# Hybrid decoder trunk: a pooled chunk moved two places, squares one chunk later, the convolution branch by column halves, attention outputs split straight from PSUM

## The chip, the cores and the metric

The kernel runs on one core of a Trainium2 chip. The metric is the time of one execution in microseconds (us), taken on the device; the figure for a kernel is the median of its runs. Beside the times there is one profiled execution, with a trace of every instruction.

## The reference

Two layers, each of a token mixer, a cross-attention into 256 memory tokens and a channel mixer (a dense SwiGLU in layer 0, a top-2-of-8 mixture of experts in layer 1); 256 tokens of width 1024, all float32. The change lies in the mixer and the attention:

```python
proj = xn @ w_in + b_in                       # conv a, b; pool; q, k, v, z; i, f; three gates
u = causal_depthwise_conv(c_a * sigmoid(c_b), conv_dw_w, conv_dw_b)      # 31 taps
y_a = silu(layer_norm(u, g, b)) @ w_conv_out
y_b = pool_mixer(p_u, pool_w, pool_scale) @ w_pool_out                   # 4 groups, each @ pool_w[g]
h = mlstm_chunkwise(q, k, v, ig, lf)                                     # 4 heads
h = h * rsqrt(mean(h * h) + EPS) * mlstm_norm_g                          # the second norm
y_c = (h * sigmoid(m_z)) @ w_mlstm_out
y = g[0] * y_a + g[1] * y_b + g[2] * y_c
x = x + y @ w_out
x = x + concat_heads(softmax(q @ k.T / 16) @ v) @ wo                     # cross-attention
```

## The kernel before

Everything is held transposed, with channels on the 128 partitions and the 256 tokens along the free dimension. Products keep float32 accuracy in three passes: each operand is split into a high part (rounded to the matmul's format) and a low part (what is left), and the helper `three` issues high by high, high by low and low by high.

The weights stream in chunks of 2048 columns per partition (1 MB). SyncE loads chunk c into `raw[c % 3]`; ScalarE copies it to `w_hi[c % 3]` (line 662, once TensorE has finished chunk c-3); VectorE subtracts to get `w_lo[c % 3]` (line 1017, the helper `lo`); TensorE multiplies it in 48 matmuls. The pooled chunk ("pw", four 128x128 blocks) has 512 columns and 12 matmuls.

The list `MIX` sets the order of the 63 chunks of a layer, the same on every engine. ScalarE and VectorE both run the loop "`split(c)`, then `post(c - 3)`", so the low part of chunk c stands in each queue ahead of all that follows from chunk c-3. The queues run strictly in order: a wait in a `post` holds up the splits behind it. The chunk numbers that matter (before): pu1 17, k3 18, z1 to z3 19 to 21, pw 22, gb0 to gb3 (gates) 23 to 26, wp0 and wp1 (pool output) 27 and 28, gc0 29, ga3 40, wc0 and wc1 (convolution output) 41 and 42, wo0 to wo3 43 to 46, xv3 58, xo0 59.

Beside the splits the queues carry:

- `conv31` on VectorE: the 31-tap convolution, doled out by the table `TAPS` over the chunks (line 1083, two instructions for each tap).
- `hidden(hd)` on VectorE, in the `post` two chunks after the scores of head hd (`SCORES` = 11, 15, 19, 23), scales the numerators into `q_t`; `hidden_squares(hd)` on ScalarE, in the same `post`, waits for it and squares `q_t` (line 733). In `post(26)` ScalarE takes the root of the sums (line 807) and VectorE normalises `q_t` (lines 1220 and 1222). `hidden_transpose` on TensorE (line 1617) comes after gc0.
- The pooled chunk: `pooling` in `post(17)` on VectorE; in `post(PW - 2)` ScalarE copies the pooled sums to `b_hi` (line 798) and VectorE makes `b_lo`, for which TensorE waits ahead of pw; in `post(PW)` VectorE scales the product (line 1210), ScalarE copies it (line 801), VectorE makes `b_lo`, and wp0 uses it.
- `merge` on VectorE: gate times branch. For wp it writes `xf` (line 1135) and frees the PSUM bank that gc0 takes. For wc it multiplies and adds (lines 1137 and 1138) once the whole chunk is done; ScalarE makes `a_hi` (line 749) and VectorE `a_lo` (`merged_lo`, signal `y_lo`). A wc chunk has four blocks of 128 rows of its input and fills two banks; wo0 reads `a_lo` in four steps of two blocks each and waits at each step for one `y_lo`.
- Attention: `x_output(hd)` on TensorE (line 1654) writes bank 7; it waits for the value chunk's copy `xv_done` (`x_value`, line 1147, which comes first in the `post`) and for `xo_done`, the copy of the previous head out of bank 7 (`x_out`, line 1162). ScalarE makes `a_hi` (line 769), VectorE `a_lo`. Heads 2 and 3 both come after xv3.

PSUM banks 0 to 3 go round by `bank_plan`; who takes a bank waits until it has been read.

Of the kernel before, what the change touches and what calls it, by code (L numbers as in the profile page):

```python
# [26 lines left out]
P = 128  # L27
T = 256
# [25 lines left out]
MIX += [("q", 2), ("z", 0), ("k", 2), ("pu", 0), ("q", 3), ("pu", 1), ("k", 3), ("z", 1), ("z", 2), ("z", 3), ("pw", 0)]  # L54
MIX += [("gb", i) for i in range(4)] + [("wp", i) for i in range(2)]
# [63 lines left out]
SCORES = (11, 15, 19, 23)  # L119
GATE_ROWS = AT["q", 0]  # L120
# [5 lines left out]
MEM_STEPS = (0, 1, 3)  # L126
CONSTS = 9
# [56 lines left out]
def trunk(nc, w, out):  # L184
    ctx = ExitStack()
    with ctx:
# [6 lines left out]
        def sig(name, mixer, ffn=0, before=0):  # L193
            return Signal(ctx, nc, name, mixer, ffn, before)
# [167 lines left out]
        ln_lo = sig("ln_lo", 1, before=1)  # L362
        y_done = sig("merged", 4)
# [16 lines left out]
        xo_done = sig("x_out_copied", HEADS)  # L380
# [273 lines left out]
        def _(act):  # L654
# [238 lines left out]
            def mixer(layer):  # L893
                if layer == 0:
                    first_norm()
                else:
                    for j in range(4):
                        act.wait_ge(h_ff.sem, h_ff.at(layer, j - 3))
                        square(layer, 0, j)
                    std(layer, 0)  # L900
# [16 lines left out]
                ahead(layer, SPL - 1)  # L917
# [94 lines left out]
        def _(dve):  # L1012
# [113 lines left out]
            def merge(layer, j, n, parts):  # L1126

                multiplied(layer, j)
                for i in range(parts):
                    dve.wait_ge(gate_done.sem, gate_done.at(layer, n + i + 1))  # L1130
                    s, q = 2 * ((n + i) % 4), (n + i) % 4
                    g, y = flat(gates[:, s:s + 2, :]), flat(xf[:, 2 * q:2 * q + 2, :])
                    last = y_done if n >= 8 else gate_used
                    if n < 4:
                        dve.tensor_tensor(y, g, bank(("chunk", j), i)[:, :], ALU.mult).then_inc(last.sem, 1)
                    else:
                        ch.link(dve.tensor_tensor(g, g, bank(("chunk", j), i)[:, :], ALU.mult))
                        dve.tensor_tensor(y, y, g, ALU.add).then_inc(last.sem, 1)
# [33 lines left out]
            def post(layer, j):  # L1172
# [45 lines left out]
                if j == SCORES[-1] + 3:  # L1218
# [100 lines left out]
            def mixer(layer):  # L1319
# [196 lines left out]
        def _(pe):  # L1516
# [141 lines left out]
            def chunk(layer, c):  # L1658
# [304 lines left out]
```

## Time and profile before

| | us |
|---|---|
| median of 3 runs (2160.7 to 2167.48) | 2162.11 |
| profiled execution, its time | 2162.14 |
| profiled execution, span of the core | 2160.3 |
| TensorE busy | 2059.6 |
| VectorE busy | 1637.2 |
| ScalarE busy | 1299.9 |

The span runs from the first to the last instruction in the trace, and the time of the same execution is 1.8 us longer. TensorE is busy in 95% of the span; its mean granted clock is 0.978 of full speed. The two mixers with their attention lie at 15 to 464 us and 664 to 1111 us.

### The profile page before, as it was taken

The numbers are of one execution on the slowest core, as the hardware profiler recorded it, in microseconds if no ns is written. First come the engines' busy times: TensorE is split into PE (matmuls) and PEld (weight loads), VectorE is DVE, ScalarE is ACT, GpSimd is POOL, SyncE is SP. The second block draws the span as 40 slices with busy tenths as digits, with TensorE's granted clock in tenths as the row PEclk, the third lists the DMA queues.
The fourth block names the chain that finished last, engine by engine and source line by source line (L and its number), as shares of the span: only waits on it lengthen the run. The fifth ranks groups of instructions, "written<-read, shape, count | busy, mean of one in ns | idle before, by whom it ended". The sixth has DMA issues, their size and how long they took to land.

```text
span 2160.3 us, 33554 instructions
## 1 busy us (share of the span) xinstructions
PE 2059.6 (95%) x12929; PEld 1871.5 (87%) x12929; DVE 1637.2 (76%) x1704; ACT 1299.9 (60%) x1133; POOL 13.2 (1%) x71
## 2 busy tenths in 40 slices
PE   8998999999998998989979999999999999999996
PEld 8988989889998988989878888888888888888885
DVE  6988656554446888656559888888988888898885
ACT  6664354343334664454337777777777777777774
POOL 0000000000000000000000000000000000000000
PEclk9998999999999999999989999999999999999998
DMA  8544445435554545445437999999999999999892
GB/s 248 176 124 161 132 155 176 151 117 181 190 176 145 167 124 161 135 152 175 139 136 285 385 325 376 330 366 353 354 373 331 376 332 367 343 366 373 328 377 91
DMA packets 309518, 526.76 MB, mean 244 GB/s; under 512 B 13566, under 2 KB 156582, under 8 KB 309414
## 3 DMA queue, kind: packets, MB, share of 16 engines
q1 hardware_dynamic: 309414, 525.29, 69.7%
q8 instruction: 75, 1.23, 0.2%
q14 instruction: 29, 0.24, 0.0%
HBM read 524.21 MB, written 1.05 MB: 243 GB/s over the span
## 4 chain that ended last, share of the span: by engine, by line
PE 80%; DVE 9%; issue 4%; ACT 4%; SPq 1%; PEldq 0%; DMA 0%; PEld 0%; DVEq 0%; ACTq 0%; POOL 0%
PE ps L1519 25%; PE ps L1521 24%; PE ps L1520 24%; DVE w_lo L1017 2%; DVE c L1083 2%; ACT w_hi L662 2%; PE ps L1839 1%; ACT w_hi L669 1%; PE ps L1913 1%; PE ps L1634 1%; DVE cacc L1067 1%; PE ps L1566 1%; PE ps L1654 1%; PE ps L1901 0%; PE ps L1902 0%
## 5 line engine op out<-in xcount | busy, mean ns | idle before, releaser
L1017 DVE TENSOR_TENSOR w_lo<-raw,w_hi 128x2048 fp32r<-128x2048 f32 x330 | 752.5, 2281 | 368.4 <-ACT w_hi L662 304.4
L1519 PE MATMUL ps<-w_hi,a_hi 128*128 128x512 f32 (+1 forms) x1472 | 566.1, 385 | 0.6 <-DVE h L1389 0.4
L1521 PE MATMUL ps<-w_hi,a_lo 128*128 128x512 f32 (+1 forms) x1472 | 560.5, 381 | 0.0
L1520 PE MATMUL ps<-w_lo,a_hi 128*128 128x512 f32 (+1 forms) x1472 | 559.7, 380 | 0.0
L662 ACT ACTIVATE w_hi<-raw 128x2048 fp32r<-128x2048 f32 x159 | 301.4, 1896 | 292.0 <-PE ps L1521 284.2
L1519 PE MATMUL ps<-a_hi,w_hi 128*128 128x256 f32 x1520 | 442.2, 291 | 24.1 <-DVE a_lo L1017 16.2
L1520 PE MATMUL ps<-a_lo,w_hi 128*128 128x256 f32 x1520 | 436.6, 287 | 0.0
L1521 PE MATMUL ps<-a_hi,w_lo 128*128 128x256 f32 x1520 | 436.1, 287 | 0.0
L669 ACT ACTIVATE w_hi<-raw 128x2048 fp32r<-128x2048 f32 x171 | 328.0, 1918 | 123.4 <-PE ps L1521 123.4
L1521 PEld LDWEIGHTS ps<-w_hi,a_lo 128*128 128x128 f32 x1472 | 276.5, 188 | 53.6
L1519 PEld LDWEIGHTS ps<-w_hi,a_hi 128*128 128x128 f32 x1472 | 276.7, 188 | 51.5 <-DVE w_lo L1017 0.8
L1519 PEld LDWEIGHTS ps<-a_hi,w_hi 128*128 128x128 f32 x1520 | 298.5, 196 | 26.3 <-issue 17.8
L1520 PEld LDWEIGHTS ps<-w_lo,a_hi 128*128 128x128 f32 x1472 | 276.8, 188 | 50.6
L1520 PEld LDWEIGHTS ps<-a_lo,w_hi 128*128 128x128 f32 x1520 | 298.4, 196 | 0.5
L1521 PEld LDWEIGHTS ps<-a_hi,w_lo 128*128 128x128 f32 x1520 | 298.0, 196 | 0.0
L1519 PE MATMUL ps<-b_hi,w_hi 128*128 128x256 f32 x744 | 214.3, 288 | 15.8 <-DVE b_lo L1017 14.7
L1521 PE MATMUL ps<-b_hi,w_lo 128*128 128x256 f32 x744 | 212.3, 285 | 0.0
L1520 PE MATMUL ps<-b_lo,w_hi 128*128 128x256 f32 x744 | 212.3, 285 | 0.0
L1519 PEld LDWEIGHTS ps<-b_hi,w_hi 128*128 128x128 f32 x744 | 144.6, 194 | 17.6 <-DVE b_lo L1017 10.7
L1017 DVE TENSOR_TENSOR w_lo<-mem_t,w_hi 128x2048 fp32r<-128x2048 f32 x56 | 128.4, 2292 | 21.7 <-ACT w_hi L669 21.6
L1520 PEld LDWEIGHTS ps<-b_lo,w_hi 128*128 128x128 f32 x744 | 144.6, 194 | 0.2
L1521 PEld LDWEIGHTS ps<-b_hi,w_lo 128*128 128x128 f32 x744 | 144.6, 194 | 0.0
(284 smaller groups left out, 2169.9 us busy)
## 6 DMA issues: line engine op xcount, KB each, us to landing
raw<-in_moe_w SPq DMA_DIRECT2D x171, 1024.0 KB, 6.6
raw<-in_w_in SPq DMA_DIRECT2D x68, 1024.0 KB, 5.2
mem_t<-in_moe_w SPq DMA_DIRECT2D x56, 1024.0 KB, 6.4
area<-in_moe_w SPq DMA_DIRECT2D x56, 1024.0 KB, 6.3
xf<-in_moe_w SPq DMA_DIRECT2D x56, 1024.0 KB, 6.0
raw<-in_ffn_w SPq DMA_DIRECT2D x33, 1024.0 KB, 5.3
raw<-in_w_mlstm_out SPq DMA_DIRECT2D x8, 1024.0 KB, 5.0
raw<-in_w_out SPq DMA_DIRECT2D x8, 1024.0 KB, 5.0
```

The costliest lines, as they stand in the source:

```text
L662: act.activation(w_hi[c % SPL][:, 0:n], raw[c % RAW][:, 0:n], ACT.Copy).then_inc(hi_done.sem, 1)
L669: act.activation(w_hi[m % SPL][:, :], e_raw[m % ERAW][:, 0:CH], ACT.Copy).then_inc(e_hi.sem, 1)
L1017: return dve.tensor_tensor(dst, whole, as_f32(hi), ALU.subtract)
L1067: ins = dve.scalar_tensor_tensor(dst, src, tap, dst, ALU.mult, ALU.add)
L1083: ins = dve.scalar_tensor_tensor(dst, src, tap, dst, ALU.mult, ALU.add)
L1519: pe.matmul(dst, wh, xh, start=start, stop=False, skip_group_check=True)
L1520: pe.matmul(dst, wh, xl, start=False, stop=False, skip_group_check=True)
L1521: return pe.matmul(dst, wl, xh, start=False, stop=stop, skip_group_check=True)
L1566: ins = pe.matmul(ps[4][:, 0:T], ones[:, :], sq[:, j % 2, i * T:(i + 1) * T], start=(j == 0 and i == 0), stop=(j == 3 and i == 1), skip_gr ...
L1634: ins = pe.matmul(ps[4 + hd % 2][:, tt * T:(tt + 1) * T], q_t[:, k, tt * P:(tt + 1) * P], k_t[:, k, :], start=(tt == 0 and e == 0), stop=( ...
L1654: ins = pe.matmul(ps[7][:, e * T:(e + 1) * T], vx[:, m, hd, e * P:(e + 1) * P], z_sig[:, 4 + 2 * (hd % 2) + m, :], start=(e == 0 and m == ...
L1839: ins = pe.transpose(ps[6][:, k * P:(k + 1) * P], act_e[g % 2][:, k * P:(k + 1) * P], ident[:, :])
```

## The change

Four edits. (1) The chunk pw moves behind gb1: z1 to z3 stay 19 to 21, gb0 and gb1 become 22 and 23, pw 24; from gb2 (25) on every chunk keeps its number. `PW` is used as before, so the two `post` parts of pw move too. (2) `hidden_squares` comes one `post` later on ScalarE (three chunks after the scores), and VectorE's normalisation one `post` later (27), while the root stays in `post(26)`. (3) wc0 and wc1 are multiplied by column halves: first all four row blocks into the first bank (signal `conv_out_half`), then all into the second. `merge_conv` merges and splits one half at a time, and on ScalarE and VectorE the `post` of a wc chunk comes ahead of the split of the chunk three later. (4) The copy from bank 7 into `xf` and its signal are gone: ScalarE copies high parts from PSUM, VectorE subtracts from PSUM. Head 3 uses bank 5 and waits for no bank; heads 1 and 2 wait for `xo_lo` of the head before.

```diff
-MIX += [("q", 2), ("z", 0), ... ("z", 1), ("z", 2), ("z", 3), ("pw", 0)]
-MIX += [("gb", i) for i in range(4)] + [("wp", i) for i in range(2)]
+MIX += [("q", 2), ("z", 0), ... ("z", 1), ("z", 2), ("z", 3)]
+MIX += [("gb", 0), ("gb", 1), ("pw", 0), ("gb", 2), ("gb", 3)] + [("wp", i) for i in range(2)]
...
             def x_out_hi(layer, hd):
-                act.wait_ge(xo_done.sem, xo_done.at(layer, hd + 1))
-                act.activation(a_hi[:, 2 * hd:2 * hd + 2, :], xf[:, 2 * hd:2 * hd + 2, :], ACT.Copy).then_inc(xo_hi.sem, 1)
+                act.wait_ge(xo_mul.sem, xo_mul.at(layer, hd + 1))
+                act.activation(flat(a_hi[:, 2 * hd:2 * hd + 2, :]), ps[X_OUT_BANK[hd]][:, :], ACT.Copy).then_inc(xo_hi.sem, 1)
...
-                if j - 2 in SCORES:
-                    hidden_squares(layer, SCORES.index(j - 2))
+                if j - 3 in SCORES:
+                    hidden_squares(layer, SCORES.index(j - 3))
...
+                    late = MIX[c - SPL][0] == "wc"
+                    if late:
+                        post(layer, c - SPL)
                     if c < N_MIX:
                         split(layer, c, chunk_len(c))
-                    post(layer, c - SPL)
+                    if not late:
+                        post(layer, c - SPL)
...
+            def merge_conv(layer, j, i):
+                for part in range(2):
+                    n = 8 + 2 * i + part
+                    s, q = 2 * (n % 4), n % 4
+                    g, y = flat(gates[:, s:s + 2, :]), flat(xf[:, 2 * q:2 * q + 2, :])
+                    done = wc_half if part == 0 else pe_chunk
+                    dve.wait_ge(done.sem, done.at(layer, i + 1 if part == 0 else j + 1))
+                    dve.wait_ge(gate_done.sem, gate_done.at(layer, n + 1))
+                    ch.link(dve.tensor_tensor(g, g, bank(("chunk", j), part)[:, :], ALU.mult))
+                    dve.tensor_tensor(y, y, g, ALU.add).then_inc(y_done.sem, 1)
+                    merged_lo(layer, q)
...
-                if j == SCORES[-1] + 3:
+                if j == HIDDEN_STD + 1:
                     dve.wait_ge(hid_std.sem, hid_std.at(layer, 1))
...
             def x_output(layer, hd):
-                if hd:
-                    pe.wait_ge(xo_done.sem, xo_done.at(layer, hd))
+                if hd in (1, 2):
+                    pe.wait_ge(xo_lo.sem, xo_lo.at(layer, hd))
...
                 elif kind == "wc":
                     pe.wait_ge(ln_lo.sem, ln_lo.at(layer, 1))
-                    project(layer, c, b_hi, b_lo, None, CB, CB)
+                    pe.wait_ge(lo_done.sem, lo_done.at(layer, c + 1))
+                    take_banks(layer, ("chunk", c))
+                    wh, wl = weights(c, CB)
+                    for part in range(2):
+                        for j in range(CB):
+                            for n in range(2):
+                                cols = slice((2 * part + n) * P, (2 * part + n + 1) * P)
+                                ins = three(bank(("chunk", c), part)[:, n * HALF:(n + 1) * HALF], wh[:, j, cols], wl[:, j, cols],
+                                            b_hi[:, CB + j, :], b_lo[:, CB + j, :], j == 0 and n == 0, j == CB - 1)
+                        ins.then_inc((wc_half, pe_chunk)[part].sem, 1)
```

What the move does to ScalarE's queue of layer 0, before, from z3 (the second pair of `z_sig` rows) to the first gate:

```order
119 L691 ACTIVATE z_sig<-ps1,par 128x256 [waits chunk_multiplied]
120 L691 ACTIVATE z_sig<-ps1,par 128x256
121 L733 ACTIVATE sgb,small<-q_t 128x256 [waits hidden_done]
122 L733 ACTIVATE sgb,small<-q_t 128x256 [waits act_chain]
123 L662 ACTIVATE w_hi1<-raw1 128x2048 [waits chunk_multiplied,raw_landed1,act_chain]
124 L801 ACTIVATE b_hi<-vb_pool 128x1024 [waits pool_scaled]
125 L662 ACTIVATE w_hi2<-raw2 128x2048 [waits chunk_multiplied,raw_landed2]
```

The same place in the changed kernel (its line numbers are 2 or more higher):

```order
118 L693 ACTIVATE z_sig<-ps1,par 128x256 [waits chunk_multiplied]
119 L693 ACTIVATE z_sig<-ps1,par 128x256
120 L664 ACTIVATE w_hi1<-raw1 128x2048 [waits chunk_multiplied,raw_landed1]
121 L693 ACTIVATE area<-ps2,par 128x256 [waits chunk_multiplied,pooled]
122 L693 ACTIVATE area<-ps2,par 128x256
123 L800 ACTIVATE b_hi<-vb_pool 128x1024 [waits pooled]
124 L735 ACTIVATE sgb,small<-q_t 128x256 [waits hidden_done]
125 L735 ACTIVATE sgb,small<-q_t 128x256 [waits act_chain]
126 L664 ACTIVATE w_hi2<-raw2 128x2048 [waits chunk_multiplied,raw_landed2,act_chain]
```

The squares of a head now stand behind the next weight split instead of ahead of it, and the copy that waits for the scaled pool product has moved down, past two more splits.

VectorE's queue of layer 0 at the two wc chunks, before; row 328 is the split of wo1:

```order
328 L1017 TENSOR_TENSOR w_lo2<-raw2,w_hi2 128x2048 [waits hi_done]
329 L1137 TENSOR_TENSOR area<-area,ps0 128x512 [waits gate_sigmoid,chunk_multiplied]
330 L1138 TENSOR_TENSOR xf<-xf,area 128x512 [waits dve_chain]
331 L1137 TENSOR_TENSOR area<-area,ps1 128x512 [waits gate_sigmoid]
332 L1138 TENSOR_TENSOR xf<-xf,area 128x512 [waits dve_chain]
333 L1017 TENSOR_TENSOR a_lo<-xf,a_hi 128x512 [waits merged_hi] x2
334 L1017 TENSOR_TENSOR w_lo0<-raw0,w_hi0 128x2048 [waits hi_done]
```

The changed kernel; row 334 is the split of wo1:

```order
328 L1153 TENSOR_TENSOR area<-area,ps0 128x512 [waits gate_sigmoid,conv_out_half]
329 L1154 TENSOR_TENSOR xf<-xf,area 128x512 [waits dve_chain]
330 L1023 TENSOR_TENSOR a_lo<-xf,a_hi 128x512 [waits merged_hi]
331 L1153 TENSOR_TENSOR area<-area,ps1 128x512 [waits gate_sigmoid,chunk_multiplied]
332 L1154 TENSOR_TENSOR xf<-xf,area 128x512 [waits dve_chain]
333 L1023 TENSOR_TENSOR a_lo<-xf,a_hi 128x512 [waits merged_hi]
334 L1023 TENSOR_TENSOR w_lo2<-raw2,w_hi2 128x2048 [waits hi_done]
335 L1153 TENSOR_TENSOR area<-area,ps2 128x512 [waits gate_sigmoid,conv_out_half]
```

The split has moved behind wc0's merges, and each low part follows its own half's merge.

## Rows read from the trace of the kernel before

**Rows 1.** The waits of TensorE, whole span: total us, times, longest us.
```profile
PE ps L1519 <- DVE a_lo L1017: 16.2, 5, 4.9
PE ps L1519 <- DVE b_lo L1017: 14.7, 3, 4.9
PE ps L1617 <- ACT area L691: 8.6, 2, 4.3
PE ps L1654 <- DVE xf L1162: 7.9, 2, 3.9
PE ps L1519 <- DVE xf L1135: 7.8, 2, 3.9
```

**Rows 2.** TensorE timeline: start, duration, instruction, count, [idle before, its releaser].
```profile
158.01 0.70 PE L1607 MATMUL ps<-vx,wdk 128*128 128x257 f32 x2 [1.01 <-DVE wdk L1113]
164.51 0.58 PE L1519 MATMUL ps<-b_hi,w_hi 128*128 128x256 f32 x1 [4.93 <-DVE b_lo L1017]
211.02 0.55 PE L1519 MATMUL ps<-a_hi,w_hi 128*128 128x256 f32 x1 [3.93 <-DVE xf L1135]
```

**Rows 3.** VectorE timeline from k3 to gc0, layer 0.
```profile
147.95 2.29 DVE L1017 TENSOR_TENSOR w_lo<-raw,w_hi 128x2048 fp32r<-128x2048 f32 x1 [3.06 <-ACT w_hi L662]
...
177.04 1.65 DVE L1210 TENSOR_SCALAR vb_pool<-ps,par 128x256 f32<-128x256 f32 x4
179.82 1.22 DVE L1017 TENSOR_TENSOR b_lo<-vb_pool,b_hi 128x1024 fp32r<-128x1024 f32 x1 [1.13 <-ACT b_hi L801]
181.62 2.29 DVE L1017 TENSOR_TENSOR w_lo<-raw,w_hi 128x2048 fp32r<-128x2048 f32 x1 [0.58 <-ACT w_hi L662]
...
200.28 2.29 DVE L1017 TENSOR_TENSOR w_lo<-raw,w_hi 128x2048 fp32r<-128x2048 f32 x1 [3.07 <-ACT w_hi L662]
...
210.20 1.28 DVE L1135 TENSOR_TENSOR xf<-area,ps 128x512 f32<-128x512 f32 x2
```

**Rows 4.** ScalarE timeline of the same stretch.
```profile
144.92 0.42 ACT L733 ACTIVATE sgb<-q_t 128x256 f32<-128x256 f32 x1 [9.69 <-DVE q_t L1123]
...
200.99 1.28 ACT L807 ACT_TABLE_LOAD   x1
202.49 1.90 ACT L662 ACTIVATE w_hi<-raw 128x2048 fp32r<-128x2048 f32 x1
```

**Rows 5.** TensorE timeline at wc0 and wo0, layer 0, then layer 1.
```profile
294.13 0.28 PE L1519 MATMUL ps<-b_hi,w_hi 128*128 128x256 f32 x1
...
307.78 0.35 PE L1519 MATMUL ps<-a_hi,w_hi 128*128 128x256 f32 x1 [1.98 <-DVE a_lo L1017]
315.19 0.39 PE L1519 MATMUL ps<-a_hi,w_hi 128*128 128x256 f32 x1 [3.03 <-DVE a_lo L1017]
...
955.29 0.35 PE L1519 MATMUL ps<-a_hi,w_hi 128*128 128x256 f32 x1 [1.98 <-DVE a_lo L1017]
962.70 0.58 PE L1519 MATMUL ps<-a_hi,w_hi 128*128 128x256 f32 x1 [4.31 <-DVE a_lo L1017]
```

**Rows 6.** VectorE timeline at the same place, layer 0.
```profile
296.34 2.29 DVE L1017 TENSOR_TENSOR w_lo<-raw,w_hi 128x2048 fp32r<-128x2048 f32 x1 [3.47 <-ACT w_hi L662]
...
307.79 0.69 DVE L1017 TENSOR_TENSOR a_lo<-xf,a_hi 128x512 fp32r<-128x512 f32 x1 [0.16 <-ACT a_hi L749]
```

**Rows 7.** ScalarE timeline: its wait for the end of wo0, layer 0 and layer 1.
```profile
319.92 1.92 ACT L662 ACTIVATE w_hi<-raw 128x2048 fp32r<-128x2048 f32 x1 [4.67 <-PE ps L1521]
...
968.22 1.92 ACT L662 ACTIVATE w_hi<-raw 128x2048 fp32r<-128x2048 f32 x1 [5.46 <-PE ps L1521]
```

**Rows 8.** VectorE timeline behind xv3, layer 0, and TensorE's wait there.
```profile
425.95 0.68 DVE L1147 COPY vx<-ps 128x512 f32<-128x512 f32 x1
426.55 0.68 DVE L1162 COPY xf<-ps 128x512 f32<-128x512 f32 x1
...
427.38 2.14 PE L1654 MATMUL ps<-z_sig,vx 128*128 128x256 f32 x7 [3.95 <-DVE xf L1162]
```

**Rows 9.** Stretches: us, busy (count) of PE, PEld, DVE, ACT, POOL, granted clock, DMA.
```profile
211.00:217.00 6.00, 5.98 (x28) 6.00 (x29) 5.45 (x8) 0.00 (x0) 0.00 (x0) 0.50 0.71 242
```

More of the change, by code:

```diff
@@ L53 @@
 MIX += [("q", 0), ("v", 0), ("k", 0), ("v", 1), ("q", 1), ("v", 2), ("k", 1), ("v", 3)]
-MIX += [("q", 2), ("z", 0), ("k", 2), ("pu", 0), ("q", 3), ("pu", 1), ("k", 3), ("z", 1), ("z", 2), ("z", 3), ("pw", 0)]
-MIX += [("gb", i) for i in range(4)] + [("wp", i) for i in range(2)]
+MIX += [("q", 2), ("z", 0), ("k", 2), ("pu", 0), ("q", 3), ("pu", 1), ("k", 3), ("z", 1), ("z", 2), ("z", 3)]
+MIX += [("gb", 0), ("gb", 1), ("pw", 0), ("gb", 2), ("gb", 3)] + [("wp", i) for i in range(2)]
 MIX += [("gc", i) for i in range(4)] + [("wm", i) for i in range(4)]
@@ L119 @@
 SCORES = (11, 15, 19, 23)
+HIDDEN_STD = SCORES[-1] + 3
 GATE_ROWS = AT["q", 0]
@@ L126 @@
 MEM_STEPS = (0, 1, 3)
+X_OUT_BANK = (7, 7, 7, 5)
 CONSTS = 9
@@ L362, in trunk @@
         ln_lo = sig("ln_lo", 1, before=1)
+        wc_half = sig("conv_out_half", 2)
         y_done = sig("merged", 4)
@@ L379, in trunk @@
         xo_mul = sig("x_out", HEADS)
-        xo_done = sig("x_out_copied", HEADS)
         xo_hi = sig("x_out_hi", HEADS)
@@ L803, in post @@
                     decay(layer, SCORES.index(j))
-                if j - 2 in SCORES:
-                    hidden_squares(layer, SCORES.index(j - 2))
-                if j == SCORES[-1] + 3:
+                if j - 3 in SCORES:
+                    hidden_squares(layer, SCORES.index(j - 3))
+                if j == HIDDEN_STD:
                     act.activation(small[:, STD:STD + 8], small[:, SS:SS + 8], ACT.Sqrt, bias=eps[:, 0:1], scale=1.0 / DH).then_inc(hid_std.sem, 1)
@@ L1132, in merge @@
                     g, y = flat(gates[:, s:s + 2, :]), flat(xf[:, 2 * q:2 * q + 2, :])
-                    last = y_done if n >= 8 else gate_used
                     if n < 4:
-                        dve.tensor_tensor(y, g, bank(("chunk", j), i)[:, :], ALU.mult).then_inc(last.sem, 1)
+                        dve.tensor_tensor(y, g, bank(("chunk", j), i)[:, :], ALU.mult).then_inc(gate_used.sem, 1)
                     else:
                         ch.link(dve.tensor_tensor(g, g, bank(("chunk", j), i)[:, :], ALU.mult))
-                        dve.tensor_tensor(y, y, g, ALU.add).then_inc(last.sem, 1)
+                        dve.tensor_tensor(y, y, g, ALU.add).then_inc(gate_used.sem, 1)
+            def merge_conv(layer, j, i):
[9 more added lines that the diff above has]
+                    merged_lo(layer, q)
             def residual(layer, j, i, done):
@@ L1161, in x_out @@
                 dve.wait_ge(xo_mul.sem, xo_mul.at(layer, hd + 1))
-                dve.tensor_copy(flat(xf[:, 2 * hd:2 * hd + 2, :]), ps[7][:, :]).then_inc(xo_done.sem, 1)
                 dve.wait_ge(xo_hi.sem, xo_hi.at(layer, hd + 1))
-                lo(a_lo[:, 2 * hd:2 * hd + 2, :], xf[:, 2 * hd:2 * hd + 2, :], a_hi[:, 2 * hd:2 * hd + 2, :]).then_inc(xo_lo.sem, 1)
+                lo(flat(a_lo[:, 2 * hd:2 * hd + 2, :]), ps[X_OUT_BANK[hd]][:, :], flat(a_hi[:, 2 * hd:2 * hd + 2, :])).then_inc(xo_lo.sem, 1)
             def merged_lo(layer, q):
@@ L1217, in post @@
                     hidden(layer, SCORES.index(j - 2))
-                if j == SCORES[-1] + 3:
+                if j == HIDDEN_STD + 1:
                     dve.wait_ge(hid_std.sem, hid_std.at(layer, 1))
@@ L1254, in post @@
                 if kind == "wc":
-                    merge(layer, j, 8 + 2 * i, 2)
-                    for q in (2 * i, 2 * i + 1):
-                        merged_lo(layer, q)
+                    merge_conv(layer, j, i)
                 if WO0 <= j < XK0:
@@ L1330, in mixer @@
                 for c in range(SPL, N_MIX + SPL):
+                    late = MIX[c - SPL][0] == "wc"
+                    if late:
+                        post(layer, c - SPL)
                     if c < N_MIX:
                         split(layer, c, chunk_len(c))
-                    post(layer, c - SPL)
+                    if not late:
+                        post(layer, c - SPL)
                     if layer == 0 and c - SPL == MEM_STEPS[0]:
@@ L1649, in x_output @@
                 pe.wait_ge(xv_done.sem, xv_done.at(layer, hd + 1))
-                if hd:
-                    pe.wait_ge(xo_done.sem, xo_done.at(layer, hd))
+                if hd in (1, 2):
+                    pe.wait_ge(xo_lo.sem, xo_lo.at(layer, hd))
                 for e in range(2):
                     for m in range(TT):
-                        ins = pe.matmul(ps[7][:, e * T:(e + 1) * T], vx[:, m, hd, e * P:(e + 1) * P], z_sig[:, 4 + 2 * (hd % 2) + m, :],
+                        ins = pe.matmul(ps[X_OUT_BANK[hd]][:, e * T:(e + 1) * T], vx[:, m, hd, e * P:(e + 1) * P], z_sig[:, 4 + 2 * (hd % 2) + m, :],
                                         start=(e == 0 and m == 0), stop=(m == 1), skip_group_check=True)
```

## The prediction

> **What bounds the kernel now.** I read the list of TensorE's waits first [rows 1]. TensorE is the bound, and its idle time is what an edit of this kind can win. The waits that bear on the change: for low parts (30.9 us in all, of which the pooled one ahead of pw and those of wo0 lie here), for the hidden transposes (8.6), for attention's copy out of bank 7 (7.9) and for the merges ahead of gc0 (7.8). The timelines place them. The mixer of layer 0 waits 1.0 us for `wdk`, 4.9 us ahead of pw and 3.9 us ahead of gc0 [rows 2]; then 2.0 and 3.0 us (layer 0) or 2.0 and 4.3 us (layer 1) in wo0 [rows 5]; then 3.95 us ahead of head 3's output [rows 8]. Together that is about 19 us a layer, 37 to 39 in all with layer 1, whose waits are alike.
>
> Next I followed each wait to its queue. From the end of the second `hidden` (147.95 - 3.06 = 144.9) to the first merge of wp0 (done at 210.9) VectorE works almost without pause: 66.0 us, with idle stretches of 3.06, 0.36, 3.06, 1.13, 0.58 and 3.07 ([rows 3] for the first, the fourth, the fifth and the last; the third is like the first and stands at 174; the 0.36 is ahead of `wdk`), 11.3 in all. So 54.7 us of work stand between those two points, and gc0 starts when it is through. The three 3-us pauses have one cause: ScalarE waits in its own queue for `hidden` (9.7 us the first time) and can begin the next split only after the squares [rows 4]. This stretch is bound by VectorE's work and these pauses; TensorE's waits at pw and gc0 are two views of one delay.
>
> **Edits 1 and 2, from k3 to gc0.** VectorE's instructions between the two points are the same ones in another order, so the new release of gc0 is 144.9 + 54.7 + the pauses that are left.
> - At each `hidden` ScalarE has split the next chunk beforehand, so the three pauses of 3.06 go. The pause of 0.36 goes too: it stood ahead of `wdk`, which VectorE reached before ScalarE's decay.
> - A new one stands behind the pooled low part. VectorE reaches that point after the work that reached up to 177.04 before [rows 3], less the pauses till then (6.5): at 144.9 + 25.7 = 170.6. The next split (gb3) needs TensorE to be done with gb1. TensorE is at the numerators at 157.0, needs 1.6 us for them (158.01 to 164.51 - 4.93 = 159.6 [rows 2]), and 5.83 us for each of gb0 and gb1 (wc0 and wc1 take 307.78 - 1.98 - 294.13 = 11.67 together [rows 5]): 170.2, and ScalarE's split adds 1.9 [rows 4]. VectorE waits until 172.1: 1.5.
> - The pooled product's pair of pauses stays: 1.13 and 0.58 [rows 3].
> - The root is taken behind the last squares, one chunk before it is needed, but the split of gc1 now stands behind both. ScalarE waits for the last `hidden`, then needs 3.06 for squares and split (the pause of before is just that) and 1.5 for table and root (200.99 to 202.49 [rows 4]): 4.6. VectorE has a split (2.2) and two taps (four instructions, about 1.6) to do meanwhile: 0.8.
>
> These make 4.0, and with three hand-overs of 0.1 each 4.3: 203.9. Walking the queue piece by piece I get 203.1 to 204, and take 203.6 against 211.0: **7.4 us a layer, 14.8 in all** (the second of the two waits ahead of gc0 is the same to 0.1 [rows 1], so layer 1 gains the same). Bounds: 6 if every hand-over costs twice as much, 9 if the pause at 172 is hidden. Nothing else moves gc0: pw needs its low part at 171.5 and has it at 171; the seven matmul chunks up to wp1 end at about 197.5. So TensorE still waits ahead of gc0, now about 6 us instead of 3.9; the pw wait has moved there and shrunk. wp0 has only two chunks of cover now instead of four: its operand comes at about 185.5, TensorE at 185.6. A wait there would come out of the one at gc0 until it passes 6 us, so I cost it at nothing. The wait of 4.3 us ahead of the hidden transposes stays whole: they need the bank of gc0, which ScalarE reads after a split that itself waits for gc0.
>
> What the granted clock does: after the wait ahead of gc0 TensorE runs at 0.50 of full speed from 211 to 217 [rows 9], and the first matmul takes 0.55 us [rows 2], against 0.35 after the shorter wait of 1.98 [rows 5]. The stall there is not removed, so I count neither gain nor loss.
>
> The Trainium skill (TensorE: Matmul & The Clock Gate, "What's actually happening") says that half rate is the default and activity releases it; by it a removed stall gives back more than its own length and a grown one costs no more than it does now. The trace agrees where it can: 0.50 in the row named. By that rule the sum would be the same here, since the stall at gc0 remains.
>
> **Edit 3, the convolution output.** wc0 starts at 294.1 and wc1 ends at 305.8 (307.78 - 1.98 [rows 5]). Before, the merges stand behind the split of wo1. After, the queue is free at 298.6 (end of the split at 296.34 [rows 6]), and wc0's first half is done at 297. A half takes 1.4 us to multiply and add, 0.1 + 0.65 on ScalarE, 0.7 for the low part: 2.85, and the next half starts 2.8 after the first. The four low parts: 301.4; 304.2; then the held-back split of wo1 (ScalarE 303.5 to 305.4, VectorE to 307.6), and 310.45 and 313.2. TensorE runs half of wo0 (24 matmuls, 2.9) to 308.7, waits to 310.6, runs a quarter (1.5) to 312.0, waits to 313.4 and is done at 314.8. Before, wo0 ended at 319.9 in layer 0 and at 968.2 in layer 1 [rows 7], 14.1 and 14.9 after wc1's end; now 9.0. The gains are 5.1 and 5.9, less what the clock takes: two waits of 1.9 and 1.3 may or may not bring half rate (in layer 0 one of 1.98 did soon after, in layer 1 it did not), 0 to 2.9, and I take 1.0. **4.1 + 4.9 = 9.0 us in all**, bounds 5 and 11. The column order costs TensorE nothing: 48 matmuls as before. The splits that are held back: wo1's is done at 307.6 and wanted at 314.8; wo2's at 316.7, wanted at 320.6, so 7 and 4 us of cover.
>
> **Edit 4, attention.** VectorE loses four copies of 0.68 us a layer [rows 8], but only one ends TensorE's wait. Head 3 also waits for its value copy, which stands ahead of the removed one in the same queue: it starts at 425.95 and ends at 426.6, and TensorE started at 427.4, just behind the end of the removed copy at 427.2. So the wait becomes 3.3 instead of 3.95: 0.6 us a layer, **1.2 in all**. Upper bound 7.9, if the wait for values were not real; lower bound 0. Heads 1 and 2 now wait for a low part instead of a copy; the copy of head 1 ended about 2 us before TensorE asked for it, and the low part now comes where that copy ended, so I cost this wait at nothing (0.7 at most, one subtraction). Reading PSUM twice is priced by the copy's 0.68 and the SBUF subtraction's 0.69 [rows 6, 8]: no difference.
>
> The Trainium skill (VectorE: DVE Perf Modes, "Rules for kernel authors") advises to copy a matmul's output to SBUF first if many operations read it, or to accept the slow rate. It speaks against this edit only if reads from PSUM were slower, and the rows named show none for float32. By it the edit would be a loss off TensorE's path, and the sum the same.
>
> **Sum.** 14.8 + 9.0 + 1.2 = 25.0. The profiled execution took 2162.14 (span 2160.3), the median is 2162.11, so no correction: 2137.
>
> **The rivals.**
> - *The bound only shifts (0.12).* The pauses on VectorE are not removed but regrouped: ScalarE's wait for the scaled pool product now holds the split of wp1, and the split of gc1 stands behind squares and root. For it: I find four pauses left, and a fifth or longer ones are easily missed. Against: none of them is as long as 3 us. Edits 1 and 2 give nothing: 2162.1 - 10.2 = 2152.
> - *The held-back split eats the convolution's gain (0.10).* The chain for the last quarter is now serial and may lag, with half rate in all of wo0. Edit 3 then gives 0: 2162.1 - 16.0 = 2146.
> - *More is won (0.08).* Attention's wait goes wholly (7.9 instead of 1.2): 2130. Against it stands the value copy in [rows 8].
> - *Slower (0.03).* wp0's operand. Two chunks of cover have gone (11.5 us), and the chain for it runs over VectorE, ScalarE and VectorE behind two splits. It decides when the operand comes more than 6 + 12.5 us later than my 185.5, since 6 are covered by the wait at gc0 and 25.0/2 is the gain of a layer; at 22 us late it would be 2169. The rows show no pause near that size on VectorE.
> - *It does nothing (0.03)*: the queues' order shows that all four edits are in place, so this needs gains and losses that cancel: 2162.
> - The forecast has 0.62, with a range of its own of 2131 to 2143; 0.02 is left for none of these.
>
> **How the numbers follow.** What a measurement of this kernel can tell from no change is about 0.3%, 6.5 us: faster means under 2155.6. The forecast and the first three rivals lie there (0.92), and most of the rest: faster 0.93, same 0.04, slower 0.03. The range of 2129 to 2149 takes in the forecast, the convolution rival and the one that wins more (0.80); the low end adds the upper bounds of edits 1 to 3 (about 5 us more) and the high end their lower ones (about 8 less) with a margin.
>
> **What would show it.** Right: no wait over 0.5 us ahead of pw or for `wdk`; a wait of 5 to 7 us ahead of gc0, which starts 7.4 us earlier in layer 0 (203.6) and as much more in layer 1; 4.3 us ahead of the transposes as before; two short waits inside wo0 (about 1.9 and 1.3) and none ahead of it; about 3.3 us ahead of head 3's output, ended by the value copy. Wrong: a wait ahead of wp0 or wp1, a pause of 3 us on VectorE between 145 and 203, or waits in wo1 and wo2 for their weights.

## The result, and the profile after

The changed kernel takes 2136.18 us (median of 4 runs, 2134.63 to 2137.52), against 2162.9 for the kernel before on the same chip; the ratio is 0.9874 (95% interval 0.9861 to 0.9888). The forecast was 2137, a gain of 25.0 against one of 26.7 measured. The profiled execution took 2137.52, its span is 2135.5, so the gain to be explained in the two traces is 24.8.

The page of the changed kernel, its span and busy times:

```profile
span 2135.5 us, 33558 instructions
PE 2055.0 (96%) x12929; PEld 1867.7 (87%) x12929; DVE 1632.6 (76%) x1696; ACT 1300.0 (61%) x1133; POOL 15.4 (1%) x71
```

TensorE's idle time fell from 2160.3 - 2059.6 = 100.7 to 80.5 us. That is 20.2 of the 24.8; the other 4.6 are busy time, in which the same 12929 matmuls took less. Its waits (total, times, longest), to be laid beside [rows 1]:

```profile
PE ps L1537 <- DVE xf L1140: 11.7, 2, 5.9
PE ps L1537 <- DVE a_lo L1023: 10.5, 5, 4.9
PE ps L1635 <- ACT area L693: 8.6, 2, 4.3
PE ps L1672 <- DVE vx L1164: 6.7, 2, 3.4
PE ps L1537 <- DVE b_lo L1023: 4.8, 1, 4.8
```

Two of the three waits for `b_lo` are gone (those ahead of pw), gc0's wait for the merges has grown, and attention's ends with the value copy. In place, on TensorE's timeline:

```profile
203.94 0.55 PE L1537 MATMUL ps<-a_hi,w_hi 128*128 128x256 f32 x1 [5.87 <-DVE xf L1140]
216.80 0.66 PE L1635 MATMUL ps<-ident,q_t 128*128 128x128 f32 x2 [4.31 <-ACT area L693]
303.25 0.39 PE L1537 MATMUL ps<-a_hi,w_hi 128*128 128x256 f32 x1 [1.72 <-DVE a_lo L1023]
306.02 0.39 PE L1537 MATMUL ps<-a_hi,w_hi 128*128 128x256 f32 x1 [1.08 <-DVE a_lo L1023]
414.69 0.76 PE L1672 MATMUL ps<-z_sig,vx 128*128 128x256 f32 x1 [3.35 <-DVE vx L1164]
...
840.41 0.55 PE L1537 MATMUL ps<-a_hi,w_hi 128*128 128x256 f32 x1 [5.87 <-DVE xf L1140]
```

VectorE's pauses from the end of the second `hidden` (144.8) to gc0, beside [rows 3]; the last row holds wp0's merges:

```profile
155.81 0.56 DVE L1119 SCALAR_TENSOR_TENSOR wdk<-ps,dec 128x384 f32<-128x384 f32 x1 [0.36 <-issue]
...
172.26 2.29 DVE L1023 TENSOR_TENSOR w_lo<-raw,w_hi 128x2048 fp32r<-128x2048 f32 x1 [1.47 <-ACT w_hi L664]
...
184.81 1.23 DVE L1023 TENSOR_TENSOR b_lo<-vb_pool,b_hi 128x1024 fp32r<-128x1024 f32 x1 [1.13 <-ACT b_hi L803]
186.62 2.29 DVE L1023 TENSOR_TENSOR w_lo<-raw,w_hi 128x2048 fp32r<-128x2048 f32 x1 [0.58 <-ACT w_hi L664]
...
196.99 2.29 DVE L1023 TENSOR_TENSOR w_lo<-raw,w_hi 128x2048 fp32r<-128x2048 f32 x1 [0.76 <-ACT w_hi L664]
...
203.11 1.28 DVE L1140 TENSOR_TENSOR xf<-area,ps 128x512 f32<-128x512 f32 x2
```

They sum to 4.30 us where there were 11.26. The difference, 6.96, and a `hidden` that ends 0.12 earlier are the 7.08 by which gc0 starts earlier.

ScalarE's wait for the end of wo0 in both layers, beside [rows 7]:

```profile
307.82 1.92 ACT L664 ACTIVATE w_hi<-raw 128x2048 fp32r<-128x2048 f32 x1 [0.77 <-PE ps L1539]
...
944.65 1.92 ACT L664 ACTIVATE w_hi<-raw 128x2048 fp32r<-128x2048 f32 x1 [0.77 <-PE ps L1539]
```

The gain can be followed by the start of the same instruction in both traces:

| point | before | after | saved so far | in this stretch |
|---|---|---|---|---|
| gc0, layer 0 | 211.02 | 203.94 | 7.08 | 7.08 |
| wc0 | 294.13 | 286.98 | 7.15 | 0.07 |
| split behind wo0 | 319.92 | 307.82 | 12.10 | 4.95 |
| output of head 3 | 427.38 | 414.69 | 12.69 | 0.59 |
| first chunk of layer 1 | 664.46 | 652.87 | 11.59 | -1.10 |
| gc0, layer 1 | 859.05 | 840.41 | 18.64 | 7.05 |
| wc0 | 941.63 | 923.81 | 17.82 | -0.82 |
| split behind wo0 | 968.22 | 944.65 | 23.57 | 5.75 |
| output of head 3 | 1075.67 | 1051.52 | 24.15 | 0.58 |
| router of the mixture | 1111.22 | 1088.62 | 22.60 | -1.55 |
| last transposes | 2151.56 | 2126.78 | 24.78 | 2.18 |

Edits 1 and 2 gave 14.1 us, edit 3 10.7, edit 4 1.2; stretches that the change doesn't touch gave back 1.2 in all. The last row holds one wait near the end that is 10.21 us long in the trace before and 6.64 in this one, so without it they would have given back 4.8.

### The profile page after: what moved, and what is told of

Its sections match the earlier page's. It is cut to its first block, busy times and chain, and to the rows that moved or that the text cites. A ratio compares the mean times of both kernels' runs of the same rounds, so it can differ in the third digit from the quotient of the medians.

```text
span 2135.5 us, 33558 instructions
## 1 busy us (share of the span) xinstructions
PE 2055.0 (96%) x12929; PEld 1867.7 (87%) x12929; DVE 1632.6 (76%) x1696; ACT 1300.0 (61%) x1133; POOL 15.4 (1%) x71
## 4 chain that ended last, share of the span: by engine, by line
PE 88%; DVE 5%; ACT 3%; issue 3%; SPq 1%; DMA 0%; DVEq 0%; ACTq 0%
PE ps L1537 27%; PE ps L1539 27%; PE ps L1538 27%; DVE w_lo L1023 1%; ACT w_hi L664 1%; PE ps L1866 1%; ACT w_hi L671 1%; PE ps L1940 1%; DVE c L1089 1%; PE ps L1652 1%; PE ps L1672 1%; PE ps L1584 1%; PE ps L1928 0%; PE ps L1929 0%; PE ps L1615 0%
## 5 line engine op out<-in xcount | busy, mean ns | idle before, releaser
L1023 DVE TENSOR_TENSOR w_lo<-raw,w_hi 128x2048 fp32r<-128x2048 f32 (+1 forms) x330 | 753.0, 2282 | 345.8 <-ACT w_hi L664 281.9
L664 ACT ACTIVATE w_hi<-raw 128x2048 fp32r<-128x2048 f32 (+1 forms) x159 | 301.5, 1897 | 318.8 <-PE ps L1539 311.0
L1537 PE MATMUL ps<-a_hi,w_hi 128*128 128x256 f32 x1520 | 439.7, 289 | 22.2 <-DVE xf L1140 11.7
L671 ACT ACTIVATE w_hi<-raw 128x2048 fp32r<-128x2048 f32 x171 | 328.4, 1920 | 123.2 <-PE ps L1539 123.2
L1539 PE MATMUL ps<-b_hi,w_lo 128*128 128x256 f32 x744 | 211.6, 284 | 0.0
L1023 DVE TENSOR_TENSOR w_lo<-area,w_hi 128x2048 fp32r<-128x2048 f32 x56 | 128.4, 2292 | 20.6 <-ACT w_hi L671 20.6
```

Source lines behind the costliest of these rows:

```text
L664: act.activation(w_hi[c % SPL][:, 0:n], raw[c % RAW][:, 0:n], ACT.Copy).then_inc(hi_done.sem, 1)
L671: act.activation(w_hi[m % SPL][:, :], e_raw[m % ERAW][:, 0:CH], ACT.Copy).then_inc(e_hi.sem, 1)
L1023: return dve.tensor_tensor(dst, whole, as_f32(hi), ALU.subtract)
L1537: pe.matmul(dst, wh, xh, start=start, stop=False, skip_group_check=True)
L1539: return pe.matmul(dst, wl, xh, start=False, stop=stop, skip_group_check=True)
```

## The experiments

Ratios are to the kernel before, in runs on the same chip, with 95% intervals. A run and the changed kernel were timed at different times, so beside the difference of their medians stands the one by the ratios. The granted clock is TensorE's, 1.00 for full speed and 0.50 for half.

**Each edit alone.** Edit 1, only the two `MIX` lines of the diff, on the kernel before.

> The pooled chunk two places later, alone. Theory (the stretch up to gc0 is VectorE's work plus the pauses that ScalarE's squares put into it): the three pauses of 3.06 us stay, so the wait ahead of pw shrinks and the wait ahead of gc0 grows by as much; gc0 starts at 210 to 212 us in layer 0, and the time is 2162 (2158 to 2165). Rival (the move itself takes the pw wait of 4.9 us with its half-rate stretch off TensorE's path): 2162 less 2 times 5 to 7 us, 2148 to 2152.

2161.84, ratio 0.9993 (0.9981 to 1.0004): no gain that the times can show. TensorE's waits ahead of pw and gc0 and VectorE's pauses, in its timelines:

```profile
177.28 0.39 PE L1519 MATMUL ps<-b_hi,w_hi 128*128 128x256 f32 x1 [2.38 <-DVE b_lo L1017]
...
211.13 0.36 PE L1519 MATMUL ps<-a_hi,w_hi 128*128 128x256 f32 x1 [2.44 <-DVE xf L1135]
```

```profile
148.04 2.29 DVE L1017 TENSOR_TENSOR w_lo<-raw,w_hi 128x2048 fp32r<-128x2048 f32 x1 [3.07 <-ACT w_hi L662]
...
173.01 2.29 DVE L1017 TENSOR_TENSOR w_lo<-raw,w_hi 128x2048 fp32r<-128x2048 f32 x1 [3.06 <-ACT w_hi L662]
...
200.38 2.29 DVE L1017 TENSOR_TENSOR w_lo<-raw,w_hi 128x2048 fp32r<-128x2048 f32 x1 [3.06 <-ACT w_hi L662]
```

The time and gc0's start (211.13) came as expected, the waits only in part: the one ahead of pw is halved (4.9 to 2.4), but the one at gc0, expected to grow, is shorter too (3.9 to 2.4). The time turns up ahead of `wdk` (2.6) and wp1 (2.2). As long as VectorE keeps its three pauses, its sum fixes gc0, and TensorE only waits in other places.

Edit 2 alone, on the kernel before:

```diff
-                if j - 2 in SCORES:
-                    hidden_squares(layer, SCORES.index(j - 2))
+                if j - 3 in SCORES:
+                    hidden_squares(layer, SCORES.index(j - 3))
...
-                if j == SCORES[-1] + 3:
+                if j == SCORES[-1] + 4:
                     dve.wait_ge(hid_std.sem, hid_std.at(layer, 1))
```

> The squares one chunk later on ScalarE and the normalisation one chunk later on VectorE, alone, with the pooled chunk where it was. Theory: the three pauses of 3.06 us go; a wait of about 1.5 us stays ahead of pw; the pauses left are the pooled product's pair (1.1 and 0.6) and at most 1 behind the root, so gc0 starts at 202 to 204 us in layer 0, as early as with both edits, and the time is 2162 - 15 = 2147 (2143 to 2150). Rival (both edits are needed, half each): gc0 at about 207 us and 2154 to 2156.

2152.96, ratio 0.9953 (0.9937 to 0.9969), 10.1 us: above the range expected and nearer the rival; gc0 starts at 206.43. The three pauses of 3.06 are gone, but VectorE's timeline shows others:

```profile
177.09 2.29 DVE L1017 TENSOR_TENSOR w_lo<-raw,w_hi 128x2048 fp32r<-128x2048 f32 x1 [1.66 <-ACT w_hi L662]
...
193.71 2.29 DVE L1017 TENSOR_TENSOR w_lo<-raw,w_hi 128x2048 fp32r<-128x2048 f32 x1 [1.02 <-ACT w_hi L662]
199.47 2.29 DVE L1017 TENSOR_TENSOR w_lo<-raw,w_hi 128x2048 fp32r<-128x2048 f32 x1 [1.88 <-ACT w_hi L662]
```

With the 0.36 and the 1.13 they make 6.05: 5.2 less than before, where both edits together take away 7.0. The first was 0.58 and holds the squares too, which now stand between the pooled copy and the split on ScalarE. The other two are splits that ScalarE begins late because TensorE, held up ahead of pw for 2.63, is late with the chunk three back, as ScalarE's timeline shows for the first of them:

```profile
191.76 1.92 ACT L662 ACTIVATE w_hi<-raw 128x2048 fp32r<-128x2048 f32 x1 [4.41 <-PE ps L1521]
```

Edits 1 and 2 together, on the kernel before (both diffs above):

> The pooled chunk and the squares together on the kernel before, without the other two edits. Theory: VectorE's pauses between the second hidden and gc0 are the 4.3 us of the changed kernel (0.36, 1.47, 1.13, 0.58, 0.76), gc0 starts 7.0 to 7.5 us earlier a layer, time 2162.5 - 14.5 = 2148 (2146 to 2151). With e2_squares at 2153 the pooled chunk is then worth about 2 us a layer only in company. Rival (the two only add): 0.9993 times 0.9953, which is 2151.

2149.4, ratio 0.9934 (0.9913 to 0.9955), 14.1 us, with gc0 at 203.73 and pauses of 0.37, 1.50, 1.12, 0.58 and 0.76: the changed kernel's. So edit 1, worth nothing alone, is worth about 4 us behind edit 2. The times do not settle this, since the intervals of the two ratios overlap and the rival that the gains only add (2151) lies within them. The traces do: gc0 of layer 0 starts at 211.02 before, 211.13 with edit 1, 206.43 with edit 2 and 203.73 with both, and in layer 1 the way from the first chunk to gc0 is 1.8 us shorter with both than with edit 2.

Edit 3 alone (the parts (3) of the diff, on the kernel before):

> The convolution branch by column halves with its merges ahead of the split, alone. Theory: TensorE enters wo0 without a wait and waits 1.7 and 1.1 us inside it, which costs no half rate; wo0 ends 9.0 us after wc1 instead of 14.1 and 14.9: 2162 - 11 = 2151 (2149 to 2154). Rival (half of the gain is lost to the clock or to the split that is held back): 2156.

2153.18, ratio 0.9955 (0.9939 to 0.997), 9.9 us by the medians. The waits in wo0 are 1.72 and 1.07, and the stretch around them shows full clock, where the kernel before, in the second line, has 0.72 at the same place (columns as in [rows 9]):

```profile
305.00:315.00 10.00, 7.21 (x58) 6.80 (x58) 7.31 (x8) 3.58 (x4) 0.26 (x2) 1.00 0.32 107
...
307.80:320.00 12.20, 9.17 (x51) 8.88 (x52) 6.84 (x8) 3.10 (x4) 0.26 (x2) 0.72 0.37 116
```

So of the 4.95 us of layer 0 only 2.2 are shorter waits (1.98 and 3.03 before, 1.72 and 1.08 in the changed kernel); the other 2.7 are half rate that is gone.

Edit 4 alone (parts (4)):

> Attention outputs split straight from PSUM, alone. Theory (the wait ahead of head 3's output ends with the value copy, which stands ahead of the removed copy): the wait is 3.35 instead of 3.95 us, 0.6 us a layer, time 2162 - 1.2, within what can be told apart from no change. Rival (the wait was the copy's): the wait goes and the time is 2154.

2161.0, ratio 0.9992 (0.9981 to 1.0003); the time cannot tell it from nothing, TensorE's timeline can:

```profile
429.28 1.19 PE L1653 MATMUL ps<-z_sig,vx 128*128 128x256 f32 x2 [3.35 <-DVE vx L1147]
```

The product of the four ratios is 0.9893, that of edits 1 and 2 together with 3 and 4 0.9882; measured 0.9874. The edits lie in different stretches and add, within the intervals.

**Which part of edit 3 wins.** The changed kernel with the column halves, but the posts of wc behind the splits:

```diff
-                    late = MIX[c - SPL][0] == "wc"
+                    late = False
```

> The changed kernel, but the two wc chunks' posts stand behind the weight split again; the column halves stay. Theory (the order of the queues is what edit 3 wins): wc0's merges begin only behind the split of wo1, which needs the end of wc0; the four low parts come at about 307.0, 309.9, 316.1 and 318.9 on the scale of the kernel before, so wo0 ends where it ended before, and edit 3's gain goes: 2148 (2144 to 2151). Rival (the halves win it): 2140 or less.

And with the posts ahead of the splits, but wc0 and wc1 multiplied whole (`project(layer, c, b_hi, b_lo, None, CB, CB)`, and `merge_conv` waits for the whole chunk):

> The changed kernel, but wc0 and wc1 are multiplied row block by row block again and merged when the whole chunk is done; their posts still stand ahead of the split. Theory: low parts at about 302.8, 305.7, 312.0 and 314.9, so wo0 waits 3.4 and 1.4 us instead of 1.7 and 1.1 and ends 1.7 us a layer later, with some half rate behind a wait of that length perhaps 2.4: 2140 (2138 to 2142). Rival (the halves win it): 2147.

2147.51 (0.994, 0.992 to 0.996) and 2139.76 (0.9897, 0.9878 to 0.9917). TensorE's waits in wo0 of layer 0, in the first

```profile
300.13 0.36 PE L1537 MATMUL ps<-a_hi,w_hi 128*128 128x256 f32 x1 [1.50 <-DVE a_lo L1023]
302.82 0.39 PE L1537 MATMUL ps<-a_hi,w_hi 128*128 128x256 f32 x1 [1.02 <-DVE a_lo L1023]
308.99 0.58 PE L1537 MATMUL ps<-a_hi,w_hi 128*128 128x256 f32 x1 [4.47 <-DVE a_lo L1023]
```

and in the second:

```profile
305.38 0.58 PE L1535 MATMUL ps<-a_hi,w_hi 128*128 128x256 f32 x1 [3.27 <-DVE a_lo L1022]
```

In layer 1 the second waits 3.26 and 1.07; the wait of about 1.4 that was expected behind the first is missing in layer 0.

Taking the order of the queues away costs 11.3 us by the medians and 14 by the ratios (their runs and those of the changed kernel were not taken together), all of edit 3; taking the halves away costs 3.6 or 5. The second cost is hardly clear of noise in the times (the intervals 0.9878 to 0.9917 and 0.9861 to 0.9888 overlap), but the traces show it: from wc0's start to the end of wo0 the second run takes 2.7 us longer than the changed kernel in layer 0 and 1.5 in layer 1, the first 6.0 and 5.8. The halves bring something only once the post stands ahead of the split.

**What still holds gc0.** Four taps moved from the chunks ahead of gc0 to those behind it:

```diff
-... 25: 2, 26: 2, 27: 2, 28: 2, 29: 3,
-             31: 3, 32: 4}
+... 25: 2, 28: 4, 29: 3,
+             31: 5, 32: 4}
```

> The changed kernel with four of the 31-tap convolution's taps (eight VectorE instructions, 3.2 us) taken out of the stretch ahead of gc0 and done behind it, where VectorE idles. Theory (gc0 starts when VectorE's work is through): gc0 starts 3.2 us earlier in each layer, its wait falls from 5.9 to 2.7, time 2136 - 6.4 = 2130, and a little less if the half-rate stretch shrinks too. Rival (the wait is ScalarE's chain from the root and the split of gc1): gc0 moves by less than 1 us and the time stays 2136.

2132.82 (0.9859, 0.9842 to 0.9875): 3.4 us by the medians, 3.2 by the ratios, half of what was expected. The times alone can't tell it from the changed kernel, whose interval overlaps; gc0's start can, 202.25 instead of 203.94. Its wait is 4.27 instead of 5.87: of the 3.3 us of work taken out, half came back as a pause of 2.33 where 0.76 was, since VectorE now reaches gc1's split still further ahead of ScalarE.

The merges of wp ahead of the split on VectorE, with the taps as they were:

```diff
-                if kind == "wp":
-                    merge(layer, j, 2 * i, 2)
...
+                    if MIX[c - SPL][0] == "wp":
+                        merge(layer, c - SPL, 2 * MIX[c - SPL][1], 2)
                     if c < N_MIX:
                         split(layer, c, chunk_len(c))
```

> The changed kernel with the two merges of each pool-output chunk put ahead of the weight split on VectorE. Same work, other order. Theory (the wait ahead of gc0 is only the place of the first merge in VectorE's queue): the merges of wp0 run at about 196 us, TensorE enters gc0 at 198.1 without a wait and at full rate, the transposes wait 4.3 to 4.9; 5.9 plus up to 2.6 us of half rate a layer, less 0.6: 2136 - 2 times 5.3 to 7.9, 2120 to 2126. Rival (VectorE's work is the bound and the wait reappears at the transposes or in gc1): at least half comes back and the time is 2130 or more.

2126.74 (0.9831, 0.9815 to 0.9847): 9.4 us better than the change (9.3 by the ratios), just short of the range expected. gc0 no longer waits, and the transposes wait 4.3 as expected; what was not foreseen is the wait of 2.29 us ahead of gc1. TensorE's timeline shows both:

```profile
208.96 3.60 PE L1635 MATMUL ps<-ident,q_t 128*128 128x128 f32 x16 [4.30 <-ACT area L693]
214.84 0.36 PE L1537 MATMUL ps<-a_hi,w_hi 128*128 128x256 f32 x1 [2.29 <-DVE k_t L1259]
```

**What holds head 3.** The post of xv3 ahead of the split, on ScalarE and VectorE:

```diff
-                    late = MIX[c - SPL][0] == "wc"
+                    late = MIX[c - SPL][0] == "wc" or MIX[c - SPL] == ("xv", 3)
```

> The changed kernel with the post of the last value chunk ahead of the split of the chunk three later, on ScalarE and VectorE. Theory (head 3's output waits for the value copy, and that copy for a split it does not need): the wait of 3.35 us falls to under 1, nothing waits in xo0 or later, time 2136 - 2 times 2.6 to 3.4 = 2130 (2128 to 2132). Rival (the split that is held back makes xo2 wait, or head 2's low part does): no gain.

2123.49 (0.982, 0.9803 to 0.9836): 12.7 us better than the change (11.7 by the ratios), twice what was expected. Heads 2 and 3 now run in one piece, and the stretch behind them at full clock, in its timeline and its windows:

```profile
409.01 3.61 PE L1672 MATMUL ps<-z_sig,vx 128*128 128x256 f32 x16
```

```profile
408.00:420.00 12.00, 12.00 (x89) 11.58 (x89) 4.37 (x4) 4.52 (x4) 0.00 (x0) 1.00 0.38 113
```

The changed kernel at the same place:

```profile
411.00:423.00 12.00, 8.64 (x51) 7.66 (x50) 4.18 (x4) 1.70 (x3) 0.00 (x0) 0.86 0.40 128
```

Fourteen hundredths of 12 us are 1.7 us of clock on top of the 3.35, so about 5 us a layer. Between the same two matmuls, from the end of wo0 to past attention's outputs, the traces differ by 5.2 us in layer 0 and 5.1 in layer 1. The rest of the 12.7 (some 2.6) falls in stretches that the edit doesn't touch.

**All of it.** Both orders together, and then with gc0's gate ahead of the split on ScalarE and five taps moved behind the numerators' gate:

```diff
-... 27: 2, 28: 2, 29: 3,
-             31: 3, 32: 4}
+... 27: 2, 30: 2,
+             31: 6, 32: 4}
```

> The changed kernel with both orders tried so far: wp's merges ahead of the next split on VectorE, and the post of xv3 ahead of the split on ScalarE and VectorE. If the two gains add: 2126.7 - 12.7 = 2114. Rival: part of either was luck with where half rate falls, and they don't add: 2118.

> The same two orders, and on ScalarE the gate of gc0 ahead of the split, and five taps of the convolution moved from the chunks gc0 and wp1 (28 and 29) to gc1 and gc2 (30 and 31). Theory: the wait ahead of the hidden transposes falls from 4.3 to 2.4 us, and gc1's wait for the gated numerators with it, since VectorE reaches them 3.9 us sooner: 3.9 us a layer, 2106 (2102 to 2110). Rival (gc1 waits on something else, the transposes' copies or the low part of its weights, and the wait only changes its place): 2113.

2117.39 (0.9797, 0.9778 to 0.9816) and 2110.36 (0.9768, 0.975 to 0.9786): by the ratios the last is 1.1% under the changed kernel. The first came out nearer the rival (2118) than the sum (2114): the two gains don't quite add. The second lies just above its range (2102 to 2110), 7.0 us under the first where 7.8 were worked out. In it TensorE's timeline has

```profile
206.67 1.94 PE L1635 MATMUL ps<-ident,q_t 128*128 128x128 f32 x16 [2.36 <-ACT area L693]
211.59 0.48 PE L1537 MATMUL ps<-a_hi,w_hi 128*128 128x256 f32 x1 [2.98 <-DVE k_t L1259]
```

The gate's move cut the transposes' wait as worked out (4.3 to 2.4), and the transposes run at full rate, 1.94 us instead of 3.60. But gc1 starts only 2.9 us sooner than with the two orders alone (214.50), not 3.9: VectorE now waits 0.95 us for ScalarE's split, which the gate stands ahead of. The run changes the gate and the taps together, so what each is worth in time is not shown.

## Why the prediction was right, and where it was off

**Edits 1 and 2.** The mechanism holds, step by step. VectorE's work between `hidden` and gc0 is the same, only the pauses count. Forecast and found: behind the pooled low part 1.5 and 1.47; 1.13 and 0.58 as they were; at gc1's split 0.8 and 0.76. The step "the pause of 0.36 goes too" failed: it is still there, in the changed kernel and in every other run of this part. It happens to be about the 0.3 that I had added for hand-overs, so that the sum of 203.9 is right to 0.04 is luck. No pause is longer than 1.5 us, and the rival that the bound only shifts is refuted. Then I took 203.6, by a walk piece by piece: the row gives 203.94, and so 7.1 us a layer, 14.1 in all instead of 14.8. The run with these two edits alone, 14.1 us faster by its medians, shows the same; edit 1 alone shows that pw's wait was a view of the same delay.

**The clock at gc0.** "Neither gain nor loss" is right for layer 0 (0.07 up to wc0). In layer 1 there were 0.82 lost behind a stall of 5.87 that was 3.9 before. At pw the stall is gone, and the stretch from 162 to 169 us shows 1.00 where it showed 0.53; by itself that brings nothing, since VectorE was the bound.

**Edit 3.** On the scale of the kernel before I had the four low parts at 301.4, 304.2, 310.45 and 313.2, with wc0 at 294.1. On VectorE's timeline of the changed kernel they end 7.3, 10.0, 16.2 and 19.0 us behind wc0's start; forecast were 7.3, 10.1, 16.35 and 19.1. The raw gains of 5.1 and 5.9 were measured as 4.95 and 5.75. What was mis-sized is the term for the clock, 1.0 us a layer: it is 0, as the window at 1.00 in the run of edit 3 alone shows; in the changed kernel 298.5 to 307.5 is at 1.00 too. So 10.7 instead of 9.0. The rival (the held-back split eats the gain) is refuted: wo1 and wo2 do not wait for their splits. Where the gain does go to nothing, in the run with the halves alone, no split is held back; there the low parts come late because they stand behind the split (the wait of 4.47).

**Edit 4.** 3.3 forecast, 3.35 found, ended by the value copy, 0.6 us a layer. The rival that the wait goes wholly needed another order of the queues: with the post of xv3 first, the copy is early and the wait is gone.

**The rest.** The slower rival is refuted by the absence of any wait ahead of wp0 or wp1. The 4.3 us ahead of the transposes stay, and the run with the gate moved confirms their cause, a split ahead of gc0's gate. What I had not costed is what the untouched stretches do: -1.10, -0.82, -1.55, +2.18. The -0.82 is the clock at gc0, above. In three more places TensorE runs longer at half rate, behind waits that the change leaves as they are or shortens. Windows, before and after: behind the wait of 4.8 us at the start of the dense part (the -1.10), behind the one at head 3 of layer 1, 3.95 and 3.35 long (the -1.55), and around the router (0.9 of the last stretch).

```profile
462.40:472.40 10.00, 10.00 (x71) 10.00 (x72) 6.10 (x9) 5.47 (x5) 0.00 (x0) 0.83 0.18 51
449.70:459.70 10.00, 9.93 (x62) 9.96 (x63) 5.70 (x8) 4.38 (x4) 0.00 (x0) 0.71 0.18 47
...
1075.70:1085.70 10.00, 10.00 (x77) 9.79 (x78) 2.35 (x4) 3.04 (x3) 0.00 (x0) 1.00 0.30 104
1051.50:1061.50 10.00, 9.98 (x64) 9.65 (x65) 1.16 (x2) 1.22 (x2) 0.00 (x0) 0.83 0.33 107
...
1105.70:1133.70 28.00, 18.20 (x93) 17.69 (x94) 17.69 (x64) 9.26 (x13) 0.00 (x0) 0.63 0.39 144
1083.00:1111.00 28.00, 19.11 (x88) 18.65 (x89) 17.80 (x64) 8.80 (x12) 0.00 (x0) 0.51 0.39 140
```

Against these stands the wait in the tail, 10.21 us before and 6.64 now. Why is open: it is 9.3 to 10.2 in three of the traces (before, edits 1 and 2 together, the order of edit 3 without the halves) and 6.6 to 6.7 in all others, those of edits 1, 2, 3 and 4 alone among them, so it is no effect of any edit that I could name. That the total came so near the forecast is therefore in part luck: edits 1 and 2 gave 0.7 less, edit 3 1.7 more, and of the 4.8 that the untouched stretches lost the tail gave back 3.6.

The run with the post of xv3 first gained about 5 us a layer in a stretch from which 3.35 us of stall went; at pw the trace shows the higher rate and no gain. The Trainium skill (TensorE: Matmul & The Clock Gate, "What's actually happening") states that half rate is the default and that activity releases it. Both traces agree with that for TensorE's rate. What I drew from it in the prediction holds in part: a removed stall gives back more than its length only where no other engine is the bound, and a grown one can cost more, as the 0.82 us of layer 1 show.

## What to carry to other kernels

Where two engines meet again and again, add up the pauses of the engine that is behind, between two fixed points: a wait taken away elsewhere comes back in another place (edit 1 alone) until one of those pauses goes, and then small moves behind it begin to pay. In a loop of "prepare what comes next, then finish what has come", look for the few steps whose result another engine stands waiting for, and finish those first: here edit 3 is worth nothing without this order, and the same move at two more places brought 17 to 19 us on top of the change. A gain worked out from a stall is right to a few us at best when half rate follows it, since the length of the half-rate stretch differs between versions whose stall is the same.

## What the runs showed of the hardware

- The same stall does not always cost the same: the 4.8 us at the dense part is followed by a mean clock of 0.83 or 0.71 in 10 us, in kernels that are alike there. At head 3 of layer 1 a stall of 3.95 was followed by 1.00, one of 3.35 in the changed kernel by 0.83.
- A stall's length did not decide whether half rate followed: behind 1.72 and 1.08 us the clock stayed at 1.00, and behind 2.44 ahead of gc0, in the run of edit 1 alone, it was 1.00 from 211.1 to 217.0. In the last run the transposes behind a stall of 2.36 took 1.94 us, the full rate, but behind the next one, of 2.98, the clock was 0.51 from 211.6 to 215.1.
- The first matmul behind a stall does not tell: in the run of edit 2 alone the one behind 3.25 us took 0.36, the clock was 1.00 from 206.4 to 207.1 and then 0.50 to 210.5.
- Reading PSUM where SBUF was read cost nothing: VectorE's subtraction of 128x512 from PSUM takes 0.68 us, that from SBUF 0.69; ScalarE's copy of 128x512 takes 0.59 from PSUM and 0.63 from SBUF.
